# A hybrid decoder step on one core: final norm by rows beside the down products, latent weights fetched earlier, loading and fill order rearranged

## The chip, the cores and the metric

One core of a Trainium2 chip runs the whole program. The metric is device microseconds of one execution; the time before is the median of three, 3236.02 us (3235.65 to 3238.68).

The engines named below are TensorE (PE, with its weight loads as PEld), VectorE (DVE), ScalarE (ACT), GpSimd (POOL) and SyncE (SP), which issues most DMAs. They run their own instruction lists and wait for each other by semaphores.

## The reference

One inference step of a two-layer decoder trunk over 1056 tokens (a prompt of 1024 and 8 samples of 4), model width 1024, all in float32:

```
x = rmsnorm-and-mix(layer 0: windowed attention and retention), then a gated MLP with a causal convolution
x = rmsnorm-and-mix(layer 1: latent attention, C), then the same kind of MLP
return rmsnorm(x, g_final), caches

C:   cq   = rmsnorm(h @ w_dq, g_q);   q = cq @ w_uq  (8 heads of 128 + 64 rope)
     kv   = h @ w_dkv;  c_kv = rmsnorm(kv[:256], g_kv);  k_rope = rope(kv[256:])
     attention over c_kv and k_rope (samples: also over a paged cache);  y = o @ w_o
MLP: u = h @ w_up;  act = silu(conv3(u[:2816])) * u[2816:];  y = act @ w_down
rmsnorm(x, g) = x / sqrt(mean(x*x) + eps) * g
```

## The kernel before

`c.xT` holds the residual stream transposed: 8 chunks (KC) of 128 features on the partitions, 1056 tokens along the row. Tokens are taken either as three tiles of 352 (TILES, `tokens_of`) or as nine blocks of 128 (BLOCKS, the last with the 32 sample tokens; `block_of`). Products of the mixers' inputs and of the MLPs are made from weights and inputs that are each split into a rounded half and a rest, three products per pair (SPLIT). The order of every engine's work is written out by hand, and a `Block` ends only when every engine has come to the end of its list.

**Loading** (`load_inputs`). Rows of x arrive by DMA in nine blocks. TensorE turns each block twice (`turn_raw` for xT, `turn_norm` for the normalised one). ScalarE squares a block with a running sum (L347), takes the root (L349), copies half of the turned block (L351) and rounds the gained block before it into `h` (L355). VectorE copies the other half (L385), takes the reciprocal, scales the rows (L389) and multiplies the turned block before it with the gain into one of two `whole` buffers (L376). GpSimd makes the rest (L366) of each rounded block. At the end TensorE turns the 44 pieces of old gates (L337), which ScalarE copies out (L358).

**End of an MLP** (`Mlp.__call__`). The down products run in 11 groups; the last runs by tiles: 24 outputs of six products each, in two banks in turn, VectorE adds each to xT (L1007). Beside them ScalarE squares the new xT (L482), GpSimd adds the squares up over chunks (L491), TensorE sums them over partitions (`next_sums.sum`, twice between the outputs, once behind them), and root and reciprocal over 128x352 give `norm.scale`.

**Latents** (`latents`). A first block (`apply_plain`) has VectorE make the normalised hT of all three tiles (L437) while SyncE loads w_dq, w_dkv, two rows of gains and a rope table, waits for them, and then issues `attention.first_loads`: the spill of xT to DRAM, the first pair's weights, three tables. A second block begins with four small products that spread the gain rows (L2099); then each of nine blocks of tokens is projected (L2107), normalised and turned.

**Attention** (`LatentAttention`). Pairs of heads run one after the other. Before a pair can score, 17 projection tiles are needed: three rope tiles (taken by VectorE: L2527, four times L2531, then an add on GpSimd), four key tiles (L2340, taken by ScalarE), six query tiles (ScalarE), four value tiles (VectorE). The first pair's tiles run ahead of everything, through six PSUM banks. Those of pair i+1 are placed between the steps of pair i, two in each of the steps 0 to 6 and one in 7 to 9, all through bank 7: `project(t)` waits until the tile before it is taken. The order within a pair is the list `TILE_KINDS`: rope, key, rope, key, rope, key, key, six queries, four values. A step scores one block of queries (L2385, L2387), masks and takes the maximum (VectorE, L2556), exponentiates (ScalarE, L2489), normalises, turns the probabilities of the step before (L2398) and weighs the values of two steps before (L2410). Copies out of the turning banks alternate between ScalarE and VectorE.

**Samples' attention** (`latent_samples`) reads pages of the cache by indirect DMA through a ring of 7 latent and 3 rotary buffers, merges the parts and ends with a product by w_uv. **The output projection** of layer 1 (`Project`) opens the second MLP call: SyncE loads w_o_c in eight chunks through two buffers, ScalarE rounds each (L603), VectorE makes the rest (L654). For layer 0 the first two chunks are loaded ahead (`early`, argument `begun`), for layer 1 not.

**Final norm** (`store_outputs`), a stage of its own: VectorE makes the normalised hT (24 instructions, L3020), TensorE turns it back to rows, eight transposes per block of tokens (L3005), ScalarE and VectorE copy the rows out (L3014, L3026), SyncE stores them (L3034).

Of the kernel before, what the change touches and what calls it, by code (L numbers as in the profile page):

```python
# [229 lines left out]
def load_inputs(c, h, mix, mixer):  # L230
# [7 lines left out]
    for size in (2 * KC * P, P, DEPTH * P, BLOCKS, BLOCKS, BLOCKS):  # L238
        ends.append(ends[-1] + size)
    assert ends[-1] <= KC * TOKENS  # L240
    whole = room[:, ends[0]:ends[1]].rearrange("p (s k t) -> p s k t", s=2, k=KC)
    gain_rows = room[0:GAINS * KC, ends[1]:ends[2]]
    tap_rows = room[0:4 * FC, ends[2]:ends[3]].rearrange("p (l n) -> p l n", l=DEPTH)
    total, root, inverse = (room[:, ends[n]:ends[n + 1]] for n in (3, 4, 5))
    junk = c.at("x_junk", [P, D_MODEL], F32, 104448 + 8192)
# [28 lines left out]
    with nc.Block() as block:  # L274
# [66 lines left out]
        def _(act):  # L341
            act.wait_ge(set_up, START + 1)
            for b in range(BLOCKS + 1):
# [17 lines left out]
        def _(pool):  # L361
            nc.gpsimd.memset(c.eps[:], EPS).then_inc(set_up, 1)
            for b in range(BLOCKS):
                n = rows_of(b)
                pool.wait_ge(rounded, START + b + 1)
                nc.gpsimd.tensor_tensor(h[:, 1, :, b * P:b * P + n], whole[:, b % 2, :, 0:n], h[:, 0, :, b * P:b * P + n].bitcast(F32), ALU.subtract).then_inc(split, 1)  # L366

        @block.vector
        def _(dve):
            def gain(b):  # L370
                n = rows_of(b)
                if b >= 2:
                    dve.wait_ge(split, START + b - 1)
                for half in range(2):
                    dve.wait_ge(norm_turned, START + 2 * b + half + 1)
                    nc.vector.tensor_tensor(whole[:, b % 2, 4 * half:4 * half + 4, 0:n], by_feature(norm_bank(b, half), n),  # L376
# [21 lines left out]
class Norm:  # L398
# [28 lines left out]
    def apply_plain(self, gain, load):  # L427


        c, nc = self.c, self.c.nc  # L430
        with nc.Block() as block:

            @block.vector
            def _(dve):
                for n in range(TILES):
                    for k in range(KC):
                        nc.vector.scalar_tensor_tensor(c.hT[:, k, tokens_of(n)], c.xT[:, k, tokens_of(n)], c.gains[:, gain, k:k + 1],  # L437
                                                       self.scale[:, n, :], ALU.mult, ALU.mult)

            @block.sync  # L440
            def _(sp):
                load(sp)
# [238 lines left out]

class Mlp:
# [2454 lines left out]
```

## Time and profile before

| | |
|---|---|
| median of three executions | 3236.02 us |
| the profiled execution | 3237.81 us |
| its span, first to last instruction | 3236.3 us |
| TensorE busy | 3000.4 us (93%) |
| VectorE / ScalarE / GpSimd busy | 1430.1 / 834.2 / 305.5 us |
| mean granted TensorE clock | 0.965 of full |

All numbers come from the profiled execution. Times in the rows are microseconds from the start of the span. A timeline row gives the start, the length, the engine, the line of the kernel, the operation, output <- input, and how many instructions are merged; a bracket gives the idle time of that engine just before and what ended it.

### The profile page before, as it was taken

The page shows a single profiled execution, that of the slowest core. Times are in us where ns is not written, and L with a number is a line of the kernel's source. Part 1 is how long each engine was busy: PE and PEld are TensorE (multiplying, and loading weights), DVE is VectorE, ACT ScalarE, POOL GpSimd, SP SyncE. Part 2 cuts the span into 40 slices and gives each one's busy share as a digit, 9 for nine tenths or more (in the row PEclk, how much of TensorE's full clock was granted, in tenths as well). Part 3 has the DMA queues.
Part 4 walks back from the last instruction along what each step waited for, and adds up shares of the span by engine and source line. Part 5 has one row for each costly group of instructions (what it writes and reads, how often), then busy time and mean ns, then how long its engine had stood idle before and what let it go on. Part 6 is the DMA issues. An engine that isn't in the chain of part 4 may idle for free. (4 is left out here: it accounts for less than half of the span.)

```text
span 3236.3 us, 49732 instructions
## 1 busy us (share of the span) xinstructions
PE 3000.4 (93%) x20246; PEld 2711.9 (84%) x20246; DVE 1430.1 (44%) x2746; ACT 834.2 (26%) x1543; POOL 305.5 (9%) x280
## 2 busy tenths in 40 slices
PE   5999999889999999999598999889898999999997
PEld 4888899679999999999464665666698999999997
DVE  3334444444544444444413334433426444444445
ACT  3434311332221211121222222233323112121113
POOL 3101122003000000000200000033021000000002
PEclk7999999899999999999798999999899999999998
DMA  5112111751888411120301000066321112111101
GB/s 171 47 59 61 39 48 44 267 215 53 298 286 309 143 39 39 39 64 1 129 1 45 14 1 1 1 248 260 111 66 53 39 39 63 41 52 39 39 27 56
DMA packets 202540, 287.01 MB, mean 89 GB/s; under 512 B 12730, under 2 KB 174356, under 8 KB 194772
## 3 DMA queue, kind: packets, MB, share of 16 engines
q1 hardware_dynamic: 193944, 176.01, 17.0%
q0 software_dynamic: 8448, 108.93, 9.2%
q8 instruction: 106, 1.74, 0.2%
q14 instruction: 42, 0.34, 0.0%
HBM read 263.42 MB, written 88.40 MB: 109 GB/s over the span
## 5 line engine op out<-in xcount | busy, mean ns | idle before, releaser
L826 PE MATMUL psum<-mlp_halves,w_up 128*128 128x352 f32 x6336 | 1019.6, 323 | 17.8 <-DVE mlp_halves L544 14.4
L826 PEld LDWEIGHTS psum<-mlp_halves,w_up 128*128 128x128 f32 x6336 | 1014.1, 189 | 21.0 <-DVE mlp_halves L544 16.2
L864 PE MATMUL psum<-acts,w_down 128*128 128x352 f32 x3168 | 516.4, 323 | 7.8 <-DVE xT L1007 6.4
L864 PEld LDWEIGHTS psum<-acts,w_down 128*128 128x128 f32 x3168 | 510.4, 189 | 10.4 <-DVE xT L1007 7.6
L1007 DVE TENSOR_TENSOR xT<-xT,psum 128x352 f32<-128x352 f32 x528 | 274.6, 521 | 238.5 <-PE psum L864 238.5
L1290 PE MATMUL psum<-h_ab,w_in_halves 128*128 128x352 f32 x2016 | 341.8, 326 | 8.7 <-POOL w_in_halves L1590 7.6
L1290 PEld LDWEIGHTS psum<-h_ab,w_in_halves 128*128 128x128 f32 x2016 | 323.0, 189 | 22.5 <-issue 10.9
L913 ACT CAST acts<-window 128x1056 fp32r<-128x1056 f32 x44 | 47.4, 1076 | 708.2 <-PE psum L864 572.3
L491 POOL TENSOR_TENSOR norm_temps<-norm_temps 128x352 f32<-128x352 f32 x72 | 76.4, 1074 | 1429.4 <-ACT norm_temps L482 1426.6
L626 PE MATMUL psum<-mlp_halves,project_w 128*128 128x352 f32 x1152 | 188.0, 326 | 13.6 <-DVE project_w L654 13.6
L626 PEld LDWEIGHTS psum<-mlp_halves,project_w 128*128 128x128 f32 x1152 | 186.7, 191 | 14.3 <-DVE project_w L654 13.9
L992 DVE TENSOR_TENSOR window<-psum,conv 128x352 f32<-128x352 f32 x132 | 67.4, 514 | 235.4 <-PE psum L826 180.5
L974 DVE TENSOR_SCALAR conv<-window,taps_sb 128x1072 f32<-128x1072 f32 x44 | 36.9, 838 | 232.7 <-ACT window L905 232.7
L752 DVE TENSOR_TENSOR w_up<-mlp_raw,w_up 128x2048 fp32r<-128x2048 f32 x44 | 100.9, 2292 | 27.7 <-ACT w_up L745 27.7
L908 ACT ACTIVATE conv<-conv 128x1072 f32<-128x1072 f32 x44 | 48.5, 1101 | 187.1 <-DVE conv L985 187.1
L1590 POOL TENSOR_TENSOR w_in_halves<-w_in_raw,w_in_halves 128x1024 fp32r<-128x1024 f32 x28 | 66.5, 2376 | 317.0 <-ACT w_in_halves L1458 317.0
L2556 DVE CUSTOM_DVE_ANT_0 xT<-psum,mla_causal 128x128 f32<-128x128 f32 (+7 forms) x64 | 46.0, 753 | 100.7 <-issue 100.6
L2870 DVE COPY hT<-psum 128x512 f32<-128x512 f32 x79 | 54.4, 691 | 80.1 <-PE psum L2764 79.5
L2764 PE MATMUL psum<-ident_sb,pages_sb 128*128 128x128 f32 x512 | 70.0, 288 | 20.1 <-DMA pages_sb<-in_cache_c_kv,page_rows_sb 18.5
L2764 PEld LDWEIGHTS psum<-ident_sb,pages_sb 128*128 128x128 f32 x512 | 57.8, 146 | 32.9 <-issue 23.0
L745 ACT CAST w_up<-mlp_raw 128x2048 fp32r<-128x2048 f32 x44 | 83.9, 1907 | 5.4 <-DMA mlp_raw<-in_w_up 5.4
L2410 PEld LDWEIGHTS psum<-xT,mla_v 128*128 128x128 f32 x576 | 66.7, 192 | 20.0 <-issue 11.7
(317 smaller groups left out, 3341.8 us busy)
## 6 DMA issues: line engine op xcount, KB each, us to landing
mlp_raw<-in_w_up SPq DMA_DIRECT2D x88, 512.0 KB, 5.1
out_new_a_k_s<-in_cache_a_k POOLq DMA_DIRECT2D x8, 4088.0 KB, 15.3
out_new_a_v_s<-in_cache_a_v POOLq DMA_DIRECT2D x8, 4088.0 KB, 15.3
mlp_raw<-in_w_down SPq DMA_DIRECT2D x22, 1024.0 KB, 6.6
w_in_raw<-in_w_in_ab SPq DMA_DIRECT2D x28, 512.0 KB, 4.6
xT<-x_spill SPq DMA_DIRECT2D x2, 4224.0 KB, 16.8
ws_k_rows<-in_cache_a_k SPq DMA_DIRECT2D x8, 1024.0 KB, 10.4
ws_v_rows<-in_cache_a_v SPq DMA_DIRECT2D x8, 1024.0 KB, 10.1
```

Source lines behind the costliest of these rows:

```text
L491: self.c.nc.gpsimd.tensor_tensor(self.gather_to[:, n, :], self.gather_to[:, n, :], self.slot(o, n), ALU.add).then_inc(norm.gathered, 1)
L626: mm = nc.tensor.matmul(c.bank[self.bank_of(o, n)][:, 0:TILE], self.weights[o % 2][:, wx, k, :], self.halves[:, x, k, tokens_of(n)], start ...
L745: self.c.nc.scalar.copy(self.w_up[s][:, 0].rearrange("p a k n -> p (a k n)"), self.raw[:, 0:2, :].rearrange("p a n -> p (a n)")).then_inc( ...
L752: self.c.nc.vector.tensor_tensor(lo, self.raw[:, 0:2, :].rearrange("p a n -> p (a n)"), hi.bitcast(F32), ALU.subtract).then_inc(self.up_sp ...
L826: mm = nc.tensor.matmul(c.bank[TILES * part + n][:, 0:TILE], w_up[s][:, w, part, k, :], h[:, x, k, tokens_of(n)], start=k + w + x == 0, st ...
L864: mm = nc.tensor.matmul(c.bank[6 + t % 2][:, 0:TILE], w_down[:, w, s, o * P:(o + 1) * P], acts[s][:, x, tokens_of(n)], start=s + w + x == ...
L992: nc.vector.tensor_tensor(product(s)[:, n * TILE:n * TILE + m], c.bank[TILES + n][:, 0:m], conv[s][:, n * TILE:n * TILE + m], ALU.mult).th ...
L1007: nc.vector.tensor_tensor(x, x, c.bank[6 + t % 2][:, 0:TILE], ALU.add).then_inc(self.added, 1)
L1290: mm = nc.tensor.matmul(c.bank[tile_bank(t)][:, 0:TILE], halves[ch % 2][:, x, j, :], h[:, y, j, tokens_of(n)], start=j + x + y == 0, stop= ...
L1590: nc.gpsimd.tensor_tensor(halves[ch % 2][:, 1].rearrange("p k n -> p (k n)"), raw[:, ch % 2].rearrange("p k n -> p (k n)"), halves[ch % 2] ...
L2410: mm = nc.tensor.matmul(c.bank[6][:, e * P:(e + 1) * P], v[i % 2][:, kb, e, :], probs_T[:, score_index(i, b, e) % 4, kb, :], start=kb == 0 ...
L2764: mm = nc.tensor.transpose(bank_of(u)[:, j * P:(j + 1) * P], keys, c.ident[:])
```

## The change

Six edits, in several places of the program:

- `load_inputs`: three `whole` buffers instead of two (at a place of their own), and ScalarE rounds block b-2, not b-1, behind its copy of block b.
- The first MLP's SyncE loads w_dq and w_dkv (`LatentWeights`) once the last up product is done, ahead of the conv stores.
- `latents` is one block. SyncE loads the gain rows and the rope table, waits for the table, and issues `first_loads`. TensorE waits for weights and gain rows, and per block for the tiles that it reads. VectorE normalises tile 0, copies the spread gains, normalises tile 1, and tile 2 when it comes to block 2.
- `TILE_KINDS`: the four keys first, then query and rope in turn, then the other queries and the values. The second weight buffers and some scratch of the attention lie elsewhere.
- `latent_samples`: two of the seven latent buffers and the rotary ring lie where w_dq and w_dkv lay; SyncE loads the first two chunks of w_o_c there (`project.early`) after the fourth product of the merge.
- The final norm goes by rows inside the second MLP (`FinalRows`): raw xT is turned to rows, blocks 0 to 4 between the last down outputs, 5 to 8 behind them; ScalarE squares and scales rows, GpSimd multiplies blocks 0 to 4 with the gain, VectorE scales and gains blocks 5 to 8 in one instruction. The norm's sums over squares, the long reciprocals and the stage `store_outputs` are gone.

```diff
 load_inputs
+    WHOLES = 3
+    whole = c.at("x_whole", [P, WHOLES, KC, P], F32, 112640)
 ...
-            for b in range(BLOCKS + 1):
+            for b in range(BLOCKS + 2):
 ...
-                if b >= 1:
-                    n = rows_of(b - 1)
-                    act.wait_ge(gained, START + 2 * b)
-                    nc.scalar.copy(h[:, 0, :, (b - 1) * P:(b - 1) * P + n], whole[:, (b - 1) % 2, :, 0:n]).then_inc(rounded, 1)
+                if b >= 2:
+                    n = rows_of(b - 2)
+                    act.wait_ge(gained, START + 2 * (b - 1))
+                    nc.scalar.copy(h[:, 0, :, (b - 2) * P:(b - 2) * P + n], whole[:, (b - 2) % WHOLES, :, 0:n]).then_inc(rounded, 1)
 ...
-                if b >= 2:
-                    dve.wait_ge(split, START + b - 1)
+                if b >= WHOLES:
+                    dve.wait_ge(split, START + b - WHOLES + 1)
 Mlp, SyncE
                     groups(sp, body)
+                    if ahead:
+                        sp.wait_ge(self.up_ready, START + (self.chunk0 + FC) * TILES)
+                        ahead(sp)
                     sp.wait_ge(self.tail_taken, START + FILLED * (call + 1))
 ...
                     sp.wait_ge(self.stored, START + 32 * (call + 1))
+                    if final:
+                        final.store(sp)
 Mlp, last down products
+                            if last and final:
+                                if t in final.TURN_AT:
+                                    if t == KC:
+                                        pe.wait_ge(self.tail_taken, START + FILLED * (call + 1))
+                                    final.turn(pe, final.TURN_AT[t], (self.added, START + (LAST_GROUP + group0) * OUTS))
 ...
+                    if final:
+                        for b in range(final.EARLY, BLOCKS):
+                            final.turn(pe, b, (self.added, START + (LAST_GROUP + group0) * OUTS))
 ...
+                        for b in range(BLOCKS):
+                            final.take_root(act, b)
+                            if b == 1:
+                                final.move(act, 0)
+                                final.move(act, 1)
+                            if b in (3, 4):
+                                final.move(act, b - 1)
+                            if b == 4:
+                                final.move(act, 4)
 FinalRows
+    EARLY = 5
+    TURN_AT = {8: 0, 10: 1, 16: 2, 18: 3, 20: 4}
+    INVERT_AT = {11: 0, 13: 1, 19: 2, 21: 3, 23: 4}
+    def rows(self, b):
+        return self.c.scores[b % 3][0:rows_of(b), :]
+    def turn(self, pe, b, added):
+        c, nc = self.c, self.c.nc
+        pe.wait_ge(added[0], added[1] + KC * ((b * P + rows_of(b) - 1) // TILE + 1))
+        if 3 <= b < 3 + self.EARLY:
+            pe.wait_ge(self.moved, START + b - 2)
+        elif b >= 3 + self.EARLY:
+            pe.wait_ge(self.finished, START + b - 2 - self.EARLY)
+        for k in range(KC):
+            mm = nc.tensor.transpose(self.rows(b)[:, k * P:(k + 1) * P], c.xT[:, k, block_of(b)], c.ident[:])
+        mm.then_inc(self.turned, 1)
+    def take_root(self, act, b):
+        act.wait_ge(self.turned, START + b + 1)
+        nc.scalar.activation(self.junk[0:rows_of(b), :], self.rows(b), ACT.Square, accum_out=self.of(self.total, b)).then_inc(self.squared, 1)
+        act.wait_ge(self.squared, START + b + 1)
+        nc.scalar.activation(self.of(self.root, b), self.of(self.total, b), ACT.Sqrt, bias=self.c.eps[0:rows_of(b), :],
+                             scale=1.0 / D_MODEL).then_inc(self.rooted, 1)
+    def finish(self, dve, b):
+        self.c.nc.vector.scalar_tensor_tensor(self.y[0:rows_of(b), b, :], self.rows(b), self.of(self.inverse, b), self.g[0:rows_of(b), :],
+                                              ALU.mult, ALU.mult).then_inc(self.finished, 1)
 latents
+                sp.dma_start(g_rows[:, 0:C_Q], d["g_q"]).then_inc(g_in, 16)
+                sp.dma_start(g_rows[:, C_Q:], d["g_kv"]).then_inc(g_in, 16)
+                sp.dma_start(rope[:], d["mla_rope"]).then_inc(rope_in, 16)
+                sp.wait_ge(rope_in, START + 16)
+                attention.first_loads(sp)
                 sp.wait_ge(normed, START + BLOCKS)
 ...
+                        pe.wait_ge(applied, START + KC * ((b * P + rows_of(b) - 1) // TILE + 1))
 ...
+                norm.apply_plain(0, 1, applied)
                 for h in range(2):
                     dve.wait_ge(g_ready, START + h + 1)
                     nc.vector.tensor_copy(g[:, 320 * h:320 * h + 320], c.bank[4 + h][:, 0:320]).then_inc(g_taken, 1)
+                norm.apply_plain(1, 1, applied)
 ...
+                    if b == 2:
+                        norm.apply_plain(2, 1, applied)
 LatentAttention
-        TILE_KINDS = [kind for n in range(TILES) for kind in (("rope", 0, n), keys[n])] + keys[TILES:]
-        TILE_KINDS += [("q", e, n) for e in range(2) for n in range(TILES)] + [("v", 0, n) for n in range(4)]
+        TILE_KINDS = keys + [kind for n in range(TILES) for kind in (("q", 0, n), ("rope", 0, n))]
+        TILE_KINDS += [("q", 1, n) for n in range(TILES)] + [("v", 0, n) for n in range(4)]
 latent_samples, SyncE
+                sp.wait_ge(merge_pe, START + 4)
+                project.early(sp, w_out)
 trunk
-            mlp(0, d["w_out_ab"][0], mix, 2, project, norm, 1, True, roll)
+            mlp(0, d["w_out_ab"][0], mix, 2, project, norm, 1, True, roll, latent_weights.load)
 ...
-            mlp(1, d["w_o_c"][0], mix, 3, project, norm, 2, False)
-        with c.hidden("hT2"), c.stage():
-            store_outputs(c, norm)
+            mlp(1, d["w_o_c"][0], mix, 3, project, norm, 2, True, ahead=final.load, final=final)
```

## Rows read from the trace of the kernel before

**Rows 1.** The page, span in 40 slices: TensorE's busy tenths, its granted clock

```profile
PE   5999999889999999999598999889898999999997
...
PEclk7999999899999999999798999999899999999998
```

**Rows 2.** Timeline of the loading stage: start us, length us, instruction, idle before

```profile
18.20 0.75 DVE L389 TENSOR_SCALAR x_rows<-x_rows,mix 128x1024 f32<-128x1024 f32 x1
...
31.64 1.05 ACT L347 ACTIVATE x_junk<-x_rows 128x1024 f32<-128x1024 f32 x1
31.81 2.35 POOL L366 TENSOR_TENSOR h_ab<-mix,h_ab 128x1024 fp32r<-128x1024 f32 x1 [2.90 <-ACT h_ab L355]
...
33.02 0.57 ACT L351 COPY xT<-psum 128x512 f32<-128x512 f32 x1
...
33.34 1.37 DVE L389 TENSOR_SCALAR x_rows<-x_rows,mix 128x1024 f32<-128x1024 f32 x1
34.63 1.27 DVE L376 TENSOR_TENSOR mix<-psum,gains_sb 128x512 f32<-128x512 f32 x2
...
35.83 0.67 DVE L385 COPY xT<-psum 128x512 f32<-128x512 f32 x1
35.94 1.04 ACT L355 CAST h_ab<-mix 128x1024 fp32r<-128x1024 f32 x1 [2.36 <-DVE mix L376]
...
36.52 1.91 PE L307 MATMUL psum<-ident_sb,x_rows 128*128 128x128 f32 x8
...
51.60 0.27 DVE L385 COPY xT<-psum 128x128 f32<-128x128 f32 x1
...
54.35 1.37 DVE L389 TENSOR_SCALAR x_rows<-x_rows,mix 32x1024 f32<-32x1024 f32 x1
...
61.54 0.81 ACT L358 COPY old_gates<-psum 128x352 f32<-128x352 f32 x2 [3.23 <-PE psum L337]
```

**Rows 3.** Timeline from the first MLP's end to the first latent product

```profile
1578.60 11.99 DVE L437 SCALAR_TENSOR_TENSOR hT<-xT,gains_sb,norm_scale 128x352 f32<-128x352 f32 x24 [1.99 <-PEq L193]
...
1603.30 0.43 SPq L2218 DMA_DIRECT2D mla_causal<-in_causal  x1
...
1604.17 2.47 PE L2099 MATMUL psum<-lat_g_rows,ones_sb 1*128 1x320 f32 x4 [30.54 <-PEq L431]
...
1606.57 7.60 PE L2107 MATMUL psum<-w_dq_sb,hT 128*128 128x384 f32 x16
```

**Rows 4.** Timeline of the end: last down products, final norm

```profile
3177.67 9.88 PE L864 MATMUL psum<-acts,w_down 128*128 128x352 f32 x60 [0.68 <-DVE acts L1000]
...
3207.51 0.52 DVE L1007 TENSOR_TENSOR xT<-xT,psum 128x352 f32<-128x352 f32 x1 [0.90 <-PE psum L864]
...
3215.50 11.99 DVE L3020 SCALAR_TENSOR_TENSOR hT<-xT,gains_sb,norm_scale 128x352 f32<-128x352 f32 x24 [0.96 <-PEq L193]
...
3227.54 3.28 PE L3005 MATMUL psum<-ident_sb,hT 128*128 128x128 f32 x28 [0.21 <-DVE hT L3020]
...
3230.85 0.68 DVE L3026 COPY y_rows<-psum 32x512 f32<-32x512 f32 x1 [0.18 <-PE psum L3005]
```

**Rows 5.** Timeline of the attention, pair 0, steps 0 to 3

```profile
1741.86 0.68 PE L2385 MATMUL psum<-mla_k,mix 128*128 128x128 f32 x4 [0.99 <-DVE mla_v L2535]
...
1745.51 2.12 DVE L2531 TENSOR_TENSOR mla_by<-psum,mla_sin 32x352 f32<-32x352 f32 x4
...
1747.69 3.58 PE L2340 MATMUL psum<-cT,w_uk 128*128 128x512 f32 x4 [1.94 <-DVE mla_by L2531]
...
1758.03 0.45 PE L2398 MATMUL psum<-ident_sb,xT 128*128 128x128 f32 x1 [2.22 <-DVE mla_w_ukT L2447]
...
1768.91 1.98 PE L2340 MATMUL psum<-cT,w_uk 128*128 128x512 f32 x4 [2.31 <-DVE mla_by L2531]
...
1770.73 1.88 PE L2385 MATMUL psum<-mla_k,mix 128*128 128x512 f32 x4
```

**Rows 6.** Timeline of the second output projection's first rounding

```profile
2328.78 1.04 ACT L603 CAST project_w<-project_raw 128x1024 fp32r<-128x1024 f32 x1 [4.25 <-DMA project_raw<-in_w_o_c]
```

More of the change, by code:

```diff
@@ L425, in split_up, with apply_plain @@
         return NormSplit(self, gain, halves, whole, self.splits - 1, self.sums - 1)
-    def apply_plain(self, gain, load):
+    def apply_plain(self, n, gain, done):
         c, nc = self.c, self.c.nc
[L431 to L442, printed above, removed]
+        for k in range(KC):
+            nc.vector.scalar_tensor_tensor(c.hT[:, k, tokens_of(n)], c.xT[:, k, tokens_of(n)], c.gains[:, gain, k:k + 1],
+                                           self.scale[:, n, :], ALU.mult, ALU.mult).then_inc(done, 1)
 class NormSums:
@@ L753, in rest_up, with __call__ @@
                                        ALU.subtract).then_inc(self.up_split, 1)
-    def __call__(self, layer, w_out, mix, gain, project, norm, restored, begun, beside=None):
+    def __call__(self, layer, w_out, mix, gain, project, norm, restored, begun, beside=None, ahead=None, final=None):
         self.prepare(layer)
@@ L778, in __call__ @@
         split = norm.split_up(gain, h, whole)
-        next_sums = norm.sum_up(temps[1][:], True)
+        next_sums = None if final else norm.sum_up(temps[1][:], True)
         project.begin(w_out, mix, h, project_weights, sums)
@@ L958, in _ @@
                         beside(pool)
-                    for n in range(TILES):
-                        for o in range(1, KC - 1):
-                            next_sums.gather(pool, o, n)
+                    if final:
+                        for b in range(final.EARLY):
+                            final.gain(pool, b)
+                    else:
+                        for n in range(TILES):
+                            for o in range(1, KC - 1):
+                                next_sums.gather(pool, o, n)
                 @block.vector
@@ L1034, in _ @@
                     add(LAST_GROUP, True)
-                    next_sums.invert(dve, TILES - 1)
+                    if final:
+                        for b in range(final.EARLY, BLOCKS):
+                            final.invert(dve, b)
+                            final.finish(dve, b)
+                    else:
+                        next_sums.invert(dve, TILES - 1)
 def flat(ap):
@@ L3092, in trunk @@
                     with c.stage():
-                        latents(c, norm, cqT, cT, krT, c_rows, kr, c_stored, attention)
+                        latents(c, norm, latent_weights, cqT, cT, krT, c_rows, kr, c_stored, attention)
                     with c.stage():
```

207 lines of the change are left out of this document (108 added, 99 removed).

## The prediction

> **What bounds the kernel now.** The first view to read is the span in 40 slices [rows 1]. TensorE (the row PE) is 90% busy or more in most slices, and there the kernel is bound by products that this change doesn't touch: the two MLP stages. So I look for slices where the digit falls, and for each I read the timeline and ask which wait ends last. There are five such places that the change touches: the first slice (loading the input), the slices around 1600 us (start of the latents), those from 1740 to 1940 us (attention of the prompt), the end of the samples' attention at 2330 us, and the last 30 us. PEclk falls to 7 or 8 tenths in slices of that kind: around a pause TensorE runs for a while at 1.2 instead of 2.4 GHz, so a removed pause can give back more than its own length.
>
> **A, loading.** Now, for each block of 128 rows, the work goes round one loop between two engines [rows 2]: ScalarE squares block b (31.64) and takes the root, VectorE scales it (33.34) and then gains block b-1 (34.63), and only after that gain can ScalarE round block b-1 (35.94) and begin the next square. VectorE's copies at 35.83 (block 5) and 51.60 (block 8) stand three blocks apart: 5.26 us each. The change makes ScalarE round block b-2 and gives the whole products a third buffer, so the rounding waits for a gain of the round before, which is done. What is late next: VectorE with copy 0.67, scale 1.37, gain 1.27 and about 0.2 for the reciprocal, 3.5 us; ScalarE with 1.95 from the square to the end of its copy and 1.04 for rounding, 3.0; GpSimd 2.35; TensorE with two turns of 8 transposes at 1.91 each at the low clock, 3.8, and about half of that at the high one. I take 3.5, since a busier TensorE should hold the high clock at least in part. Six periods (blocks 3 to 8) give 6 x 1.76 = 10.6. At the end, block 8's scale starts 2.75 us after its copy (51.60, 54.35), because its square stood behind a rounding; about 0.7 remain, so 2.0 more. The turns of the old gates that end the stage (to 62.35) follow that scale, and move with it. Sum -12.6. Ends: -8.8 with 3.8 us a block and no gain at the end, -15.6 with ScalarE's 3.0.
>
> Here a rule can be weighed. The scale takes 0.75 us at 18.20 and 1.37 at 33.34, where a GpSimd subtraction began 1.53 us earlier; the scale ends at 34.71, 0.55 after GpSimd's 34.16, and block 8's row repeats this [rows 2]. The Trainium skill, SBUF — State Buffer, section "SBUF: two separate sides", says that such a VectorE instruction and a GpSimd one hold a shared port pair in turn, the first for its whole length while the other blocks; the trace fits that. By that rule, a scale that starts ahead of GpSimd would take 0.75, and the block 3.0 instead of 3.5 us, so A would be -15.6 and the time 3153. By the row alone it stays 1.37, since the subtraction would still fill two thirds of the period. I keep the row.
>
> **B, start of the latents.** Now VectorE normalises all three tiles (24 instructions, 11.99 us from 1578.60) while SyncE loads weights. Then TensorE still stands until 1604.17, because both are a block of their own whose end waits for SyncE, and SyncE issues the attention's first loads until 1603.73 [rows 3]. Afterwards four small products spread the gains, and the first latent product starts at 1606.57. The change loads the two weights behind the last up products of the first MLP, some 30 us of down products before they are wanted (the second MLP's down stage, 3177.67 to 3208 [rows 4], has the same shape), so they are hidden; uncovered, all that SyncE does here took 25 us, and that is the upper bound. Two conv stores are queued behind them there, with the same cover. The extra block is gone, and TensorE waits only for tile 0 and the gain rows: 1578.6 + 8 x 0.50 = 1582.6 for the tile; for the rows two issues of about 0.4 and at most 4.7 (what lies between the last copy at 3231.53 and the span's end at 3236.3, a store's whole way), so 1583.5; four spreading products 2.4: start at about 1585.7, -20.9. VectorE's copies of the gains stand behind tile 0, and tile 1 behind them; a block's products take 7.6 us for the first half alone, so tiles 1 and 2 (4 us each) are ready before blocks 2 and 5 want them. First loads and spill are issued beside products and nobody joins them. Ends: -12.0 if TensorE in effect waits for all three tiles (1590.6 + 2.4 + 0.5 = 1593.5, and 1.1 lost on the way), -22 if the rows land in 2 us.
>
> **C, fill tiles of the attention.** Beside each of the first three pairs of heads run the next pair's 17 projections, all through one PSUM bank, so each waits until the one before is taken. Now the first are rope, key, rope, key, rope, key. A rope tile is taken by VectorE with one product of about 0.5 and four in 2.12 us, and three TensorE waits end on it: 1.94 at 1747.69, 2.22 at 1758.03 (there the copy of w_uk stands behind the rope on VectorE) and 2.31 at 1768.91 [rows 5]. The key tile after the first runs 3.58 us against 1.98 for the same four products at 1768.91, at the low clock; the one after the second is slowed about as much. So 6.5 of waits and 3.0 of low clock lie in the 28.9 us from 1741.86 to 1770.73. The pairs that start at 1840.86 and 1939.8 repeat these rows to 0.1 us. With keys first, their takers are ScalarE copies of about 0.6 us. I charge 0.9 back for a key tile that waits for ScalarE behind the exponentials. The ropes come as the second tile of steps 2 to 4, and behind each follows a step's score and weighing on TensorE (1.88 at 1770.73 for a half of the key scores alone, about 4 us in all, an estimate), which covers 2.65. 3 x 8.6 = -25.8. Ends: 0 if the waits only move to the later steps, -28.5 if all is won. The first pair's own 17 tiles run through six banks with TensorE busy: 0.
>
> **D, output projection.** ScalarE waits 4.25 us for the first weights [rows 6], and TensorE's first product stands behind it. They now load while the samples are merged: -4.2; ends -3 and -4.4.
>
> **E, final norm.** Now, after the last add (3208.03), come a sum, root and reciprocal, a stage opening, 24 products of VectorE from 3215.50, turns and copies to 3231.53 [rows 4]. New: 24 outputs at 0.97 (60 matmuls in 9.88 are ten of them) are 23.4, and five turned blocks of 8 transposes at 0.117 (28 in 3.28) are 4.7, with no sum products and no long reciprocal between the adds: end of the products 3205.8, of the last add 3206.4. Behind it: turn of block 5 1.0, ScalarE still scaling block 4 0.4, square and root 1.4 (31.64 to 33.02 [rows 2]), reciprocal 0.3, VectorE's product 1.4 (11.99 / 24 for 352 wide, so 1.45 for 1024), then block 8, whose banks wait for that product: 1.0 + 1.4 + 0.3 + 1.45. That is 8.7, end 3215.1: -16.4. The five gains on GpSimd (2.35 each) end before block 5 does. Ends: -12 with turns at the low clock and a wait for ScalarE in each, -18.5 if the stores end sooner too, being spread.
>
> Ten semaphores more are set up at the start: +0.5, from 0 to 1 (a stage with five of them opens within the 0.96 us in the bracket of 3215.50 [rows 4]).
>
> **Sum.** -12.6 - 20.9 - 25.8 - 4.2 - 16.4 + 0.5 = -79.4. The profiled execution took 3237.81 (span 3236.3, 1.5 around it), so 3158.4. It lies 1.8 above the median of 3236.02; so I predict 3156.6, say 3156. From the ends, without C at zero: -50 to -89, 3147 to 3186.
>
> **Rivals.**
> 1. The rope waits only move: in steps 2 to 4 the next block's masking queues behind the rope on VectorE, and TensorE waits there. For it: three ropes cost the same VectorE time anywhere. Against: from step 3 the score alone outlasts them. C is 0: 3182.
> 2. The latents wait for the whole norm or for a slow gain row: B is -12: 3165. For it: VectorE takes the tile's work and the gains in one queue. Against: only tile 0 stands ahead.
> 3. The last down products are stretched by the turned blocks and ScalarE's chain runs past them, so that the final norm keeps half its tail: E is -8: 3165.
> 4. In A the scale comes ahead of GpSimd's subtraction and takes 0.75 us, as at 18.20 [rows 2]: 3153. For it: ScalarE's rounding, which releases GpSimd, now waits for the gain of the round before. Against: from block 2 on, the old loop has no such scale. (It is what the Trainium skill's port rule, cited at A, would bring.)
> 5. Slower: the pauses removed are TensorE's only rests, and without them its granted clock falls inside an MLP stage. Product work that takes 1 us at 2.4 GHz costs 1 us more at 1.2. The two MLPs fill about 20 of 40 slices, 1600 us; from 80 us of that, one twentieth, the gain is eaten, and with 90 us the time is 3246. Against it: PEclk shows 9 in the slices without a pause and falls only with pauses [rows 1].
> 6. The change does not do what it says (loads or norm stand where they stood): 3236.
>
> **Chances.** Forecast 0.70 (its own range 3146 to 3172), rival 1 0.10, 2 0.06, 3 0.05, 4 0.04, 5 0.03, 6 0.02. I take 3145 to 3184, which leaves out rivals 5 and 6 and the far tails. A measurement here tells about 0.2% (6.5 us) from no change: faster 0.95, same 0.02, slower 0.03.
>
> **What would show it.** A: copies of block 5 to 8 about 3.5 us apart and the stage's end near 50. B: a pause of about 10 us instead of 30 between the last sum product and the first latent product. C: no TensorE wait over 1 us on the rope's rows in pairs 0 to 2. D: no DMA wait at the first rounding. E: under 10 us from last add to last VectorE product. The prediction is wrong if the sum of these stands in the trace and the time does not follow it, or if PEclk falls in the MLP slices.

## The result, and the profile after

The changed kernel takes 3144.14 us (median of four executions, 3142.08 to 3145.00) against 3235.84 of the kernel before (median of four): ratio 0.9718, interval 0.9701 to 0.9735. Run once more beside the last experiment it took 3141.32 (five, 3139.3 to 3143.2; ratio 0.9709, 0.9696 to 0.9723). The forecast was 3156, with a range from 3145: the direction was right and the waits named in it went away, but the gain was larger than the range allowed, by 0.9 us in the first set and by 3.7 in the second.

The profiled execution took 3144.01 (span 3142.5), 93.8 us less of span than before. Between the same marks in both traces:

| from mark to mark | before | after | difference | forecast |
|---|---|---|---|---|
| A: start to the mixer's first DMA (set-up in it) | 65.58 | 49.27 | -16.3 | -12.1 |
| mixer, output projection, first MLP | 1513.02 | 1511.99 | -1.0 | 0 |
| B: VectorE's norm to the first latent product | 27.97 | 4.11 | -23.9 | -20.9 |
| latents, to the first score of pair 0 | 135.29 | 135.28 | 0 | 0 |
| C: prompt attention, to the samples' first product | 372.25 | 343.29 | -29.0 | -25.8 |
| D: samples, to the projection's first product | 217.03 | 209.80 | -7.2 | -4.2 |
| projection and second MLP, to the last down products | 846.53 | 848.87 | +2.3 | 0 |
| E: to the end of VectorE's last instruction | 53.86 | 36.71 | -17.2 | -16.4 |
| last store | 4.77 | 3.18 | -1.6 | 0 |

The page's TensorE rows of after, which answer to [rows 1]: the first slice is 6 instead of 5, and the 5 of the latents' start is gone.

```profile
PE   6999999789999999999898999799899999999998
...
PEclk8999999899999999999899999999899999999999
```

The loading stage of after, a timeline as in [rows 2]:

```profile
24.94 1.06 ACT L348 ACTIVATE x_junk<-x_rows 128x1024 f32<-128x1024 f32 x1
25.11 2.60 POOL L367 TENSOR_TENSOR h_ab<-x_whole,h_ab 128x1024 fp32r<-128x1024 f32 x1 [0.18 <-ACT h_ab L356]
...
26.32 0.57 ACT L352 COPY xT<-psum 128x512 f32<-128x512 f32 x1
...
26.60 0.67 DVE L386 COPY xT<-psum 128x512 f32<-128x512 f32 x1
26.79 1.05 ACT L356 CAST h_ab<-x_whole 128x1024 fp32r<-128x1024 f32 x1
...
27.38 0.89 DVE L390 TENSOR_SCALAR x_rows<-x_rows,mix 128x1024 f32<-128x1024 f32 x1
27.73 1.06 ACT L348 ACTIVATE x_junk<-x_rows 128x1024 f32<-128x1024 f32 x1
27.91 2.60 POOL L367 TENSOR_TENSOR h_ab<-x_whole,h_ab 128x1024 fp32r<-128x1024 f32 x1 [0.19 <-ACT h_ab L356]
28.18 1.27 DVE L377 TENSOR_TENSOR x_whole<-psum,gains_sb 128x512 f32<-128x512 f32 x2
...
38.13 1.28 DVE L390 TENSOR_SCALAR x_rows<-x_rows,mix 32x1024 f32<-32x1024 f32 x1
...
40.34 4.85 PE L338 MATMUL psum<-ident_sb,mix 16*128 16x16 f32 x44
...
49.27 0.39 SPq L1347 DMA_DIRECT2D alibi_table<-in_alibi  x1
```

A block now takes 2.79 us (24.94 to 27.73), not 3.5. The scale starts at 27.38, while GpSimd's subtraction of the block before is still in its last third of a microsecond (25.11 + 2.60 = 27.71), and ends at 28.27, 0.56 behind that end. Before it started 1.53 us after a subtraction's start, and ended 0.55 behind the subtraction's end too [rows 2]: same distance, other phase. The next subtraction, released at 27.91, has become 0.25 longer. ScalarE's row has no gap left: from square to square it needs 2.79.

The start of the latents after [rows 3]: TensorE's pause is 6.7 us instead of 30.5, the gain rows land 1.1 us after their second issue ends, and the first latent product follows two things that now end together: the four spreading products (1562.87 + 2.47 = 1565.34) and VectorE's norm of tile 0 (1561.26 + 4.05 = 1565.31), which releases its weight load (PEld).

```profile
1561.26 4.05 DVE L432 SCALAR_TENSOR_TENSOR hT<-xT,gains_sb,norm_scale 128x352 f32<-128x352 f32 x8 [2.15 <-PEq L193]
1561.52 0.24 SPq L2221 DMA_DIRECT2D lat_g_rows<-in_g_kv  x1
...
1562.87 2.47 PE L2236 MATMUL psum<-lat_g_rows,ones_sb 1*128 1x320 f32 x4 [6.73 <-DMA lat_g_rows<-in_g_kv]
...
1565.37 0.50 PEld L2245 LDWEIGHTS psum<-w_dq_sb,hT 128*128 128x128 f32 x2 [0.96 <-DVE hT L432]
1565.37 7.59 PE L2245 MATMUL psum<-w_dq_sb,hT 128*128 128x384 f32 x16
```

Attention of the prompt: the groups of key products and of turned probabilities in the three pairs with fill tiles, first of before, then of after (line, operation, count; busy, mean ns of one; idle before and what ended it). The key tiles' 12.8 us of waiting for ropes and the 6.7 for the copy of w_uk are gone, and a key product takes 611 ns instead of 813. (The two windows are 298 and 290 us long and cut the steps at different places, so the counts of turned products differ.)

```profile
L2340 PE MATMUL psum<-cT,w_uk 128*128 128x512 f32 x48 | 32.3, 813 | 12.8 <-DVE mla_by L2531 12.8
L2398 PE MATMUL psum<-ident_sb,xT 128*128 128x128 f32 x216 | 31.0, 277 | 13.6 <-DVE mla_w_ukT L2447 6.7 <-ACT xT L2454 5.9 <-ACT mla_w_ukT L2447 1.0
```

```profile
L2540 PE MATMUL psum<-ident_sb,xT 128*128 128x128 f32 x236 | 33.0, 275 | 7.7 <-ACT xT L2596 5.9 <-ACT mla_w_ukT L2589 1.8
L2482 PE MATMUL psum<-cT,w_uk 128*128 128x512 f32 x48 | 23.4, 611 | 0.0
```

That the 813 was clock, two windows of before show, the key tiles of 1747.69 and 1768.91 in [rows 5]: four products each in 3.58 and 1.98 us, at a granted clock (behind the busy time) of 0.55 and of 1.00, the high level. In the changed kernel the mean clock from 1700.65 to 1990 us, where the key tiles run, is 1.00.

```profile
1747.69:1751.27 3.58, 3.58 (x5) 0.55 0.00 0
1768.91:1770.89 1.98, 1.98 (x5) 1.00 0.00 0
```

At the output projection ScalarE's first weight rounding waits for no DMA any more [rows 6], and it starts behind the cast ahead of it. At the end [rows 4], VectorE's last product ends 8.4 us after the last add (3130.96 to 3139.32); 8.7 was forecast.

```profile
2251.17 1.04 ACT L594 CAST project_w<-project_raw 128x1024 fp32r<-128x1024 f32 x1
```

```profile
3130.44 0.52 DVE L1121 TENSOR_TENSOR xT<-xT,psum 128x352 f32<-128x352 f32 x1 [0.44 <-PE psum L954]
...
3131.01 2.84 PE L716 MATMUL psum<-ident_sb,xT 128*128 128x128 f32 x24 [0.61 <-DVE xT L1121]
...
3138.05 1.27 DVE L751 SCALAR_TENSOR_TENSOR y_rows<-psum,final_inverse,final_g 32x1024 f32<-32x1024 f32 x1
```

The +2.3 us of the second MLP are clock. Two windows each, the start of the projection and the stretch behind the norm, with the granted clock behind the five busy times: 0.94 and 1.00 before, 0.90 and 0.93 after, for the same kind of products. It is no more than executions differ by: in ten other runs of the changed code there, the way from the projection's first product to the end of the last down product takes 874.6 to 877.5 us, against 876.3 before and 876.7 here.

```profile
2331.14:2360.00 28.86, 28.86 (x171) 28.86 (x172) 14.86 (x17) 10.90 (x15) 2.41 (x2) 0.94 0.19 57
2450.00:2475.00 25.00, 22.01 (x138) 21.72 (x137) 19.84 (x23) 14.05 (x22) 4.02 (x6) 1.00 0.25 71
```

```profile
2253.74:2282.60 28.86, 28.86 (x165) 28.86 (x166) 14.68 (x16) 10.68 (x15) 1.48 (x1) 0.90 0.18 55
2372.60:2397.60 25.00, 22.18 (x130) 21.89 (x129) 19.88 (x23) 14.43 (x22) 4.83 (x6) 0.93 0.16 43
```

### The profile page after: what moved, and what is told of

It reads as the page before. It is cut to its first block and busy times, and to the rows that moved or that the text cites. A ratio compares the mean times of both kernels' runs of the same rounds, so it can differ in the third digit from the quotient of the medians.

```text
span 3142.5 us, 49591 instructions
## 1 busy us (share of the span) xinstructions
PE 2975.9 (95%) x20234; PEld 2698.4 (86%) x20234; DVE 1407.1 (45%) x2727; ACT 830.1 (26%) x1535; POOL 302.2 (10%) x267
## 5 line engine op out<-in xcount | busy, mean ns | idle before, releaser
L482 POOL TENSOR_TENSOR norm_temps<-norm_temps 128x352 f32<-128x352 f32 x54 | 59.5, 1117 | 686.5 <-ACT norm_temps L473 685.1
L2631 ACT ACTIVATE xT<-xT,mla_neg_max 128x128 f32<-128x128 f32 (+7 forms) x64 | 49.2, 769 | 152.9 <-DVE mla_neg_max L2698 152.9
L2908 PE MATMUL psum<-ident_sb,pages_sb 128*128 128x128 f32 x512 | 69.1, 285 | 18.8 <-DMA pages_sb<-in_cache_c_kv,page_rows_sb 17.7
## 6 DMA issues: line engine op xcount, KB each, us to landing
out_new_a_k_s<-in_cache_a_k POOLq DMA_DIRECT2D x8, 4088.0 KB, 15.6
```

The source lines that it names most:

```text
L482: self.c.nc.gpsimd.tensor_tensor(self.gather_to[:, n, :], self.gather_to[:, n, :], self.slot(o, n), ALU.add).then_inc(norm.gathered, 1)
L2908: mm = nc.tensor.transpose(bank_of(u)[:, j * P:(j + 1) * P], keys, c.ident[:])
```

## The experiments

The theory: the parts add, each at the size between its marks, and the forecast was short because it priced waits and lengths by rows of a loop whose phase the change moves. Its rivals are told with each run. Stretches of the program that no edit touches differ between executions by up to 6 us (last section), so a part is read from its own stretch, and the whole time is given beside it. The kernel before, run beside the three groups of experiments, took 3236.51 (seven), 3233.05 (one) and 3235.71 us (nine).

**Loading put back.** The old order and two buffers in the changed kernel:

```diff
-    WHOLES = 3
+    WHOLES = 2
...
-                if b >= 2:
-                    n = rows_of(b - 2)
+                if b >= 1:
+                    n = rows_of(b - 1)
...
```

> The changed kernel with the loading put back (two whole buffers, ScalarE rounds block b-1). Theory 1, the part is worth what stands between its marks in the two traces (the mixer's first DMA 16.3 us earlier, 0.65 of set-up on top): about 17 us slower than the changed kernel, 3161, the scale at 1.37 us again and the blocks 5.26 us apart. Theory 2, the part is worth the forecast's 12.6 and the rest of the surplus has another source: 3157, and the mixer's first DMA near 62 us. Theory 3, what loading wins is partly given back later as low clock: under 10 us.

Measured: 3159.73 us (3157.04 to 3164.70), 15.6 and 18.4 above the two medians of the changed kernel; mixer's first DMA at 66.37, 17.1 later. The scale takes 1.37 again, begun 1.53 us into a subtraction, and blocks are 5.25 us apart. Theory 1 holds, and theories 2 and 3 fall: this part alone is 4.5 us more than forecast, and the whole time moves with it.

```profile
27.36 2.35 POOL L367 TENSOR_TENSOR h_ab<-x_whole,h_ab 128x1024 fp32r<-128x1024 f32 x1 [2.91 <-ACT h_ab L356]
28.89 1.37 DVE L390 TENSOR_SCALAR x_rows<-x_rows,mix 128x1024 f32<-128x1024 f32 x1
```

**The order without the third buffer, and the third buffer without the order.** The first has `WHOLES = 2` alone of the diff above, the second its other lines alone.

> The changed kernel with two whole buffers instead of three; ScalarE still rounds block b-2. Theory 1, the order is what counts: in the changed kernel's trace GpSimd's subtraction of a block ends at 30.51 and the next gain but one into that buffer would start at 30.97, so two buffers do as well: blocks 2.79 us apart, mixer's first DMA at 49.3, time as the changed kernel's within 1 us. Theory 2, the third buffer is needed: gains wait for the subtraction, blocks 3.3 us or more apart, mixer's first DMA after 52.

> The changed kernel with three whole buffers, but ScalarE rounds block b-1 again. Theory 1, the order is what counts: blocks 5.26 us apart as before, scale 1.37, mixer's first DMA at 66. Theory 2, the third buffer carries part of it: blocks under 4.5 us apart.

Measured: with the order alone blocks are 2.79 us apart, mixer's first DMA at 48.91 (49.27 with both), time 3138.54 (one execution; 5.6 and 2.8 below the changed kernel's medians, more than the 1 us expected, and 4.9 of it lies in untouched code, from the mixer to the latents: 1507.1 us against 1512.0). With the buffer alone the scale takes 1.37, blocks are 5.25 apart, mixer's first DMA at 66.17, time 3161.95 (one). All of A is the order of ScalarE's list; the third buffer buys nothing. The steady loop of the first, then of the second:

```profile
24.82 2.53 POOL L367 TENSOR_TENSOR h_ab<-x_whole,h_ab 128x1024 fp32r<-128x1024 f32 x1 [0.26 <-ACT h_ab L356]
...
27.61 2.53 POOL L367 TENSOR_TENSOR h_ab<-x_whole,h_ab 128x1024 fp32r<-128x1024 f32 x1 [0.26 <-ACT h_ab L356]
```

```profile
32.41 2.35 POOL L367 TENSOR_TENSOR h_ab<-x_whole,h_ab 128x1024 fp32r<-128x1024 f32 x1 [2.90 <-ACT h_ab L356]
...
33.94 1.37 DVE L390 TENSOR_SCALAR x_rows<-x_rows,mix 128x1024 f32<-128x1024 f32 x1
...
37.66 2.35 POOL L367 TENSOR_TENSOR h_ab<-x_whole,h_ab 128x1024 fp32r<-128x1024 f32 x1 [2.90 <-ACT h_ab L356]
```

**Each rest made twice**, to tell taking turns from running slower side by side:

```diff
+    twice = c.sem("x_twice")
...
+                nc.gpsimd.tensor_tensor(h[:, 1, :, b * P:b * P + n], whole[:, b % WHOLES, :, 0:n], h[:, 0, :, b * P:b * P + n].bitcast(F32), ALU.subtract).then_inc(twice, 1)
+                pool.wait_ge(twice, START + b + 1)
                 nc.gpsimd.tensor_tensor(h[:, 1, :, b * P:b * P + n], whole[:, b % WHOLES, :, 0:n], h[:, 0, :, b * P:b * P + n].bitcast(F32), ALU.subtract).then_inc(split, 1)
```

> The changed kernel in which GpSimd makes each rest of the loading twice, one after the other (2.36 us more per block). Theory 1, VectorE's scale and GpSimd's subtraction take turns, each holding the other off for its whole length: every scale ends 0.55 us after the end of a subtraction, whenever it began, so its duration varies between 0.75 and over 2 us; the blocks come 5.2 us apart or a little more (two subtractions of 2.36, one scale of 0.55). Theory 2, beside a subtraction the scale just runs slower: it takes 1.37 us each time, and GpSimd alone sets 4.9 us a block. The whole kernel is some 15 to 20 us slower than the changed one by either.

Measured: 3159.15 us (one). The timeline of its steady loop:

```profile
32.91 2.34 POOL L368 TENSOR_TENSOR h_ab<-x_whole,h_ab 128x1024 fp32r<-128x1024 f32 x1
...
34.97 0.83 DVE L393 TENSOR_SCALAR x_rows<-x_rows,mix 128x1024 f32<-128x1024 f32 x1
35.33 2.69 POOL L370 TENSOR_TENSOR h_ab<-x_whole,h_ab 128x1024 fp32r<-128x1024 f32 x1
37.98 2.35 POOL L368 TENSOR_TENSOR h_ab<-x_whole,h_ab 128x1024 fp32r<-128x1024 f32 x1
```

The scale ends at 35.80, 0.55 after the subtraction's end at 35.25, and the subtraction behind it takes 2.69 instead of 2.34: they take turns. A block takes 5.07 us, two subtractions of 2.34 and some 0.4 of a scale. Theory 2 (1.37 each time, 4.9 a block) falls. Of theory 1 one sentence failed: the scale's length didn't vary, since the gain ahead of it waits for GpSimd (2.25 us ahead of the gain at 38.05) and so brings it to the seam between two subtractions each time. A rival that this run alone would leave, that the scale is slowed in proportion to the time that both run, falls with the phases of the changed kernel's trace: begun 2.25 us into a subtraction of 2.60 the scale takes 0.89, begun 1.84 into one of 2.56 (block 8) it takes 1.28, and each time it ends 0.55 behind the subtraction.

**Fill order put back, and a third order.** The first has the old list; the second only turns each query and rope about, so that the rope is the first tile of its step and the query waits behind it:

```diff
-        TILE_KINDS = keys + [kind for n in range(TILES) for kind in (("q", 0, n), ("rope", 0, n))]
+        TILE_KINDS = keys + [kind for n in range(TILES) for kind in (("rope", 0, n), ("q", 0, n))]
```

> The changed kernel with the old order of the fill tiles (rope, key, rope, key, ...). Theory 1, the waits on the rope and the low clock behind them come back in full: 9.6 us for each of three pairs, 28.8 in all, 3173. Theory 2, the forecast's size: 8.6 a pair, 25.8, 3170. Theory 3 (rival 1 of the prediction), the order only moves the waits and the gain came from the attention's other edits: within 3 us of 3144.

> The changed kernel, in whose fill order each rope stands ahead of its query (keys first, then rope, query, rope, query, ...), so that in steps 2 to 4 a query's products wait behind the rope in the one bank. Theory 1, what counts is that the rope is the second tile of its step, with score and weighing behind it: the waits come back, 1.9 to 2.3 us three times in three pairs, 6.5 a pair and up to 3 of low clock: 3163 to 3173. Theory 2, what counts is that keys come first and ropes come later, when scores are longer: no wait over 1 us on a rope, 3144 within 3.

Measured: old order 3166.70 us (3164.29 to 3169.68), 22.6 and 25.4 above the changed kernel's medians, while the attention's stretch is 372.27 instead of 343.29, +29.0. Rope first 3174.30 (one, just above theory 1's 3163 to 3173), its stretch 374.56, +31.3. The waits of its TensorE (waited for: us in total, times, longest):

```profile
PE psum L2479 <- DVE mla_by L2673: 18.9, 9, 2.3
```

That is 6.3 us a pair, three ropes of 2.1 (6.5 in the old order), though keys come first and scores are longer. Theory 1 of the second holds: what counts is that the rope is the second tile of its step, with a score and a weighing behind it. For the size, stretch and whole time disagree by 4 to 6 us, no more than untouched stretches differ; the stretch says 9.7 a pair, theory 1 of the first.

**The two halves of the latents' start.** First, TensorE's first latent product waits for all three tiles, made in one go; second, the weights are loaded in the latents:

```diff
-                        pe.wait_ge(applied, START + KC * ((b * P + rows_of(b) - 1) // TILE + 1))
+                        pe.wait_ge(applied, START + KC * TILES)
...
                 norm.apply_plain(1, 1, applied)
+                norm.apply_plain(2, 1, applied)
...
-                    if b == 2:
-                        norm.apply_plain(2, 1, applied)
```

> The changed kernel, but TensorE's first latent product waits for all three normalised tiles, which VectorE makes in one go. Theory 1: the first latent product starts when VectorE's third tile ends, two tiles of 4.05 us behind the first and the copies, at about 1574.2 instead of 1565.4: 8.8 us slower, 3153. Theory 2: VectorE's third tile, which now stands in the way of the blocks' norms at 1589.73, is gone from there, and 3 to 4 us come back: 5 us slower, 3149. Theory 3: the longer pause also costs low clock: 10 to 12 us slower.

```diff
-            mlp(0, d["w_out_ab"][0], mix, 2, project, norm, 1, True, roll, latent_weights.load)
+            mlp(0, d["w_out_ab"][0], mix, 2, project, norm, 1, True, roll)
...
+                weights.load(sp)
                 sp.dma_start(g_rows[:, 0:C_Q], d["g_q"]).then_inc(g_in, 16)
```

> The changed kernel with w_dq and w_dkv loaded at the start of the latents instead of behind the last up products of the first MLP. Theory 1: the pause gets as much longer as the weights need, 11.4 us from the first issue to the landing of the five loads in the trace before, and the spreading products behind it: first latent product at 1575 instead of 1565.4, 9 to 10 us slower, 3153. Theory 2: the norm of tile 0 covers most of it: 5 us slower. Theory 3: with attention's first loads no longer waited for, the weights alone take over 15 us: 3160.

Measured: 3148.95 us (3147.72 to 3156.26; 4.8 and 7.6 above the changed kernel's medians) and 3148.59 (one; 4.4 and 7.3 above). From the norm's start to the first latent product 12.84 and 13.33 us instead of 4.11, so +8.7 and +9.2; to the first score of pair 0 +8.0 and +8.2, so under 1.1 comes back. By the stretches theory 1 holds in both; the whole times alone would fit the 5 us of theory 2 as well, and can't tell the two apart. The first one's wait follows, and the second's, whose bracket names the last gain row, issued behind the weights; the second weight, issued at 1559.77, took 10.1 us to land.

```profile
1570.83 5.49 PE L2245 MATMUL psum<-w_dq_sb,hT 128*128 128x384 f32 x8 [8.65 <-DVE hT L432]
```

```profile
1570.28 2.47 PE L2237 MATMUL psum<-lat_g_rows,ones_sb 1*128 1x320 f32 x4 [16.06 <-DMA lat_g_rows<-in_g_kv]
```

**All turns behind the last down products** (not shown: TensorE turns all nine blocks there, and VectorE takes all their reciprocals there):

```diff
-    TURN_AT = {8: 0, 10: 1, 16: 2, 18: 3, 20: 4}
-    INVERT_AT = {11: 0, 13: 1, 19: 2, 21: 3, 23: 4}
+    TURN_AT = {}
+    INVERT_AT = {}
```

> The changed kernel with all nine blocks turned behind the last down products instead of five of them between. Theory 1, ScalarE's chain sets the tail: the last add comes 4.4 us earlier (five turns of 0.87 gone), behind it nine squares with roots of 1.4 and five scalings of 1.06, with a turn ahead and a reciprocal and a product of VectorE behind, 20 us instead of 8.4: 7 to 8 us slower, 3152. Theory 2, TensorE or VectorE would have done the same work as fast (the turns between the products buy nothing but their place): within 2 us of 3144.

Measured: 3146.81 us (3146.20 to 3148.67); from the projection's first product to the end 897.2 instead of 888.7, +8.5 (other runs of the changed code there: 886.7 to 889.6). The whole time shows only 2.7 and 5.5 of it, against the two medians, and the first MLP, which no edit touches, was 4.4 us shorter in this trace (last section); by the stretch theory 1 holds. VectorE's last product ends 20.5 us after the last add (3122.50 to 3143.05), as theory 1 has it, and TensorE waits for ScalarE's scalings between turns:

```profile
3121.98 0.52 DVE L1122 TENSOR_TENSOR xT<-xT,psum 128x352 f32<-128x352 f32 x1 [0.44 <-PE psum L954]
...
3128.05 2.95 PE L716 MATMUL psum<-ident_sb,xT 128*128 128x128 f32 x16 [3.48 <-ACT y_rows L736]
...
3141.78 1.27 DVE L751 SCALAR_TENSOR_TENSOR y_rows<-psum,final_inverse,final_g 32x1024 f32<-32x1024 f32 x1
```

So of E's 17 us about half is the place beside the products. The other half is left for the rest of the edit, the norm by rows without the old sums, long reciprocals and stage; no run takes these apart.

**A version that goes further.** Three waits that the traces still show: the 44 turns of old gates that end the loading (4.85 us at 40.34), the gain rows, and the samples' first gather, which waits 4.37 us for page numbers. The gates of both layers lie on 32 partitions and are turned together; VectorE makes the last two rests; the gain rows are loaded with the weights, and the first block's products wait chunk by chunk; the latents load the page numbers and make row numbers of them. The core of it:

```diff
-                for f in range(FC):
-                    mm = nc.tensor.transpose(c.bank[2 + l][:, 16 * f:16 * f + 16], gate_rows[:, l, f * P:(f + 1) * P], c.ident[0:16, 0:16])
+                for f in range(11):
+                    at = 11 * x + f
+                    mm = nc.tensor.transpose(c.bank[2 + x][:, 32 * f:32 * f + 32], gate_rows[:, at * P:(at + 1) * P], c.ident[0:32, 0:32])
...
-            for b in range(BLOCKS):
+            for b in range(BLOCKS - 2):
                 n = rows_of(b)
                 pool.wait_ge(rounded, START + b + 1)
...
+                                if b == 0 and off == 0:
+                                    pe.wait_ge(applied, START + k + 1)
...
                 attention.first_loads(sp)
+                page_rows.load(sp)
...
-                pool.wait_ge(rows_ready, START + QUARTERS)
```

> The changed kernel once more, beside the version that tries three further edits, so that the two have runs of before in common. The parts of the program that no edit touches were seen to differ between executions by up to 6 us (from the mixer's first DMA to the norm of the latents: 1507.1 to 1513.0), so 3138 to 3146 is expected by every theory; its stretches A to E must repeat to 1 us.

> The changed kernel with three further edits. Loading: the old gates of both layers turned together, 22 transposes instead of 44, and the last two rests made by VectorE: mixer's first DMA 2 to 3 us earlier (the turns alone take 4.85 us now and end last). Latents: the gain rows come with the weights, and the first block's products wait for the norm chunk by chunk: first latent product 1.6 us after VectorE's first chunk instead of 4.1, so 1.5 to 2.5 us. Samples: the page numbers are loaded and turned into row numbers in the latents, so that GpSimd's first gather waits for nothing: the 4.4 us that it waits now go. Theory 1, all are on the path and add: 8 to 10 us faster than the changed kernel beside it. Theory 2, the pages' gathers are paced by their transfers, not by their first issue, and what is won at the first is lost at the next: 4 to 5 us.

Measured: the changed kernel repeats its stretches B, C, D and its tail to 0.2 us (4.11, 343.24, 209.68, 8.35), but A is 1.4 us shorter (47.83 against 49.27), more than the 1 us expected.

The version that goes further takes 3131.46 us (3125.83 to 3137.23; ratio to before 0.9677, 0.9664 to 0.9691) against 3141.32 of the changed kernel beside it: 9.9 faster, and the two ratios' intervals don't meet. By stretches: mixer's first DMA at 46.86 (49.27 in the first trace, 47.83 in the one beside it, where the 44 turns took 4.07); first latent product 2.4 instead of 4.1 us after the norm's start; the wait for the first pages 10.4 instead of 14.7:

```profile
2032.13 3.22 PE L2935 MATMUL psum<-ident_sb,pages_sb 128*128 128x128 f32 x14 [10.42 <-DMA pages_sb<-in_cache_c_kv,page_rows_sb]
```

2.4 (against the first trace; 1.0 against the second) + 1.7 + 4.2 for these, and 1.0 less in the rest of the samples: 9.3 or 7.9 in all, so theory 1 and not the 4 to 5 of theory 2. What GpSimd won at the first gather was kept. The edits were not run one by one; the sizes are those of their stretches.

## Why the prediction was right, and where it fell short

Of the signs named in advance four held: a pause of 6.7 us (about 10 forecast), no TensorE wait over 1 us on a rope, no DMA wait at the rounding, 8.4 us of tail (under 10). The one for A did not: copies of blocks 5 to 8 are 2.79 us apart (29.38 to 37.76), not about 3.5. Rivals 1, 2 and 3 did not happen; the experiments that bring back such waits cost 31, 9 and 8.5 us. Rival 5 did not either: PEclk stays at 9 or more in the MLPs away from their norm. The sum was short by 14.4 us of span. The step that failed most is in A, the 3.5 us a block:

- **A, -16.3 with the set-up against -12.1.** "By the row alone it stays 1.37 ... I keep the row." The 1.37 was no property of the scale but of where it starts: the rest of a running subtraction and 0.55. At the new phase it is 0.89. Rival 4, at 4 in 100, was nearest, though the scale comes at a subtraction's end, not ahead of its start. The Trainium skill, SBUF — State Buffer, section "SBUF: two separate sides", has the two hold the port pair in turn for whole instructions; the traces agree, with 0.54 to 0.56 from the subtraction's end to the scale's in all thirteen profiles. The end of the range failed too: 3.0 for ScalarE was a sum of lengths, but an instruction starts some 0.1 us before the one ahead of it ends (26.32 + 0.57 and 26.79 above), and 2.79 is what it needs from start to start. VectorE's 3.5 was such a sum too: of the 0.71 us a block that it was too long, 0.48 is the scale, and most of the rest are these overlaps. What sets the 2.79 was not tested. GpSimd waits some 0.2 us for ScalarE in each block, and VectorE's period holds the stretched scale, while ScalarE runs without a wait and with its old lengths; that points to ScalarE's list.
- **B, -23.9 against -20.9.** The gain rows were bounded by a store's whole way, 4.7, and the bound was taken as the value: spreading began 1.6 us after the norm's start, not 4.9. Now the spreading ends together with tile 0's norm, so a still faster row alone would have bought nothing.
- **C, -29.0 against -25.8.** Waits (6.5 a pair) and low clock (48 key products each 0.202 us shorter, so 3.2 a pair) were right; the 0.9 a pair charged for key tiles that wait for ScalarE did not come: idle time of the keys is 0.0.
- **D, -7.2 against -4.2.** The first weights give 4.1: ScalarE's cast of the inputs, ahead of them, starts 73.3 us earlier than before (2250.19 against 2323.47), TensorE's first product 77.4. The other 3.1 were not forecast: TensorE waits 17.7 instead of 18.5 us for pages and none for one copy (0.6), and works 1.5 us less at a better clock (0.94 instead of 0.92); the eleven other runs of the changed code give 208.7 to 211.2. Why the clock is better there stays open.
- **E, -17.2 against -16.4**, the sum nearly as written; the last store's way, 1.6 shorter, stood only in the bounds.
- **Not in the sum: +2.3** in the second MLP, the spread of the clock, as above.

A, B and C lay beyond the far ends given for them (-15.6, -22, -28.5), and D's stretch beyond its -4.4, though not the part that was priced: the ends were taken from rows of the old loop too, so the range inherited the error that it should have covered. Nor is its other side, -50, what the near ends add up to with C at its value (-8.8 - 12.0 - 25.8 - 3 - 12 + 1 = -60.6).

## What to carry to other kernels

When a change moves the phase of a loop, a length read from the old loop is the price of the old meeting: take the instruction's time alone and its partner's, and work out the new meeting. Measure an engine's period from start to start, not by adding lengths. When a bound from far rows must stand for a wait, put the near end into the range as well, and try each half of an edit alone: here the order of one engine's list carried some 17 us and its extra buffer nothing.

## What the runs showed of the hardware

VectorE's scale of 128x1024 and GpSimd's subtraction wait for each other's end: the scale takes 0.75 us alone, 0.83 to 0.90 begun in the last 0.4 us of a subtraction, 1.36 to 1.38 begun 1.53 us into one of 2.35, and the subtraction 2.33 to 2.36 where it does not follow a scale and 2.46 to 2.83 behind a scale.

The first MLP, from its first up product to the norm of the latents, has the same products in all thirteen profiles, and took 787.9 to 792.3 us; from the mixer's first DMA to that norm it was 1507.1 to 1513.0. In a long one (after, 792.3) the granted clock of its first 99 us, where TensorE waits for the norm, is 0.93, in a short one (turns behind, 787.9) 0.97, with the same waits; the two windows, TensorE alone (length, busy time and products, granted clock):

```profile
768.90:867.90 99.00, 91.89 (x539) 0.93 0.66 223
```

```profile
768.90:867.90 99.00, 91.76 (x557) 0.97 0.68 226
```

In the same 99 us the short one does 18 more products, about 2.9 us of work at the 0.16 us a product of the rest of the stretch. So 3 of the 4.4 us between the two come from how soon the clock is back after the same pauses. By whole spans a single profile can't tell parts smaller than the 4 to 6 us by which untouched stretches differ.
